# First layer of a two-layer diffusion backbone: values turned by VectorE block transposes and sixteen SBUF transfers a chunk, split on GpSimd

## What is computed

```python
h = x * (1.0 + sc) + sh
hc = ctx * (1.0 + scc) + shc
q, k, v, z = jnp.split(h @ w_in[l], 4, axis=-1)
...
p = jax.nn.softmax(s, axis=-1).astype(v.dtype)
...
return (jnp.einsum('bhwij,bhiwjd->bhwd', p_loc, v_win)
        + jnp.einsum('bhwc,bhcd->bhwd', p[..., n_win:], vc))
...
out = (y * jax.nn.silu(z)) @ w_out[l]
```

## Time and profile before

| what | value |
|---|---|
| median of three runs | 1783.38 us |
| the profiled execution's own time | 1783.56 us |
| its span, first to last instruction | 1781.4 us |
| mean granted TensorE clock | 0.997 of full speed |
| TensorE matmul busy | 1747.2 us, 98% of the span |
| VectorE busy | 1276.3 us, 72% |
| ScalarE busy | 912.5 us, 51% |
| GpSimd busy | 280.0 us, 16% |
| TensorE transposes of values in layer 0 (L687) | 80, 13.5 us busy |

### The profile page before, as it was taken

How to read it: one execution, slowest core, us unless ns; L and a number is a source line. 1 busy time by engine, 2 the same in 40 slices (tenths; PEclk the granted TensorE clock), 3 DMA queues, 4 the chain that set the end, 5 groups by cost and what they waited for, 6 DMA issues and landing times. The chain is left out here.

```text
span 1781.4 us, 30430 instructions
## 1 busy us (share of the span) xinstructions
PE 1747.2 (98%) x10261; PEld 1514.9 (85%) x10261; DVE 1276.3 (72%) x2288; ACT 912.5 (51%) x1638; POOL 280.0 (16%) x245
## 2 busy tenths in 40 slices
PE   7999999999999999999999999999999999999998
PEld 3898989898889898878878889888888888898886
DVE  6677777878787868756878585775848484857658
ACT  4665655555555555640046555564647374654500
POOL 2200000000000000356341010101000010103951
PEclk9999999999999999999999999999999999999999
DMA  9614141414141413316421020202020110102243
GB/s 359 142 37 127 33 120 42 113 47 109 48 109 50 98 52 83 121 57 207 151 83 40 13 62 12 62 0 62 12 62 12 38 36 26 47 12 69 96 155 123
DMA packets 125398, 139.14 MB, mean 78 GB/s; under 512 B 85122, under 2 KB 93474, under 8 KB 125220
## 3 DMA queue, kind: packets, MB, share of 16 engines
q1 hardware_dynamic: 111524, 112.26, 20.7%
q0 software_dynamic: 11088, 16.78, 5.0%
q10 hardware_dynamic: 2736, 9.44, 1.3%
HBM read 107.06 MB, written 17.73 MB: 70 GB/s over the span
## 5 line engine op out<-in xcount | busy, mean ns | idle before, releaser
L676 PE MATMUL acc<-h_hi,w_hi 128*128 128x512 f32 (+1 forms) x1408 | 522.9, 371 | 4.4 <-DVE h_lo L597 3.0
L676 PE MATMUL acc<-h_hi,w_lo 128*128 128x512 f32 (+1 forms) x1408 | 509.1, 362 | 0.0
L676 PE MATMUL acc<-h_lo,w_hi 128*128 128x512 f32 (+1 forms) x1408 | 508.3, 361 | 0.0
L676 PEld LDWEIGHTS acc<-h_hi,w_hi 128*128 128x128 f32 x1408 | 266.2, 189 | 43.4 <-DVE h_lo L597 5.0
L676 PEld LDWEIGHTS acc<-h_hi,w_lo 128*128 128x128 f32 x1408 | 265.7, 189 | 41.9
L676 PEld LDWEIGHTS acc<-h_lo,w_hi 128*128 128x128 f32 x1408 | 266.7, 189 | 34.6
L1841 DVE TENSOR_REDUCE stats<-acc 128x1 f32<-128x1280 f32 x128 | 189.6, 1487 | 38.8 <-PE acc L1948 37.3
L1757 ACT ACTIVATE far_pt<-acc 128x512 f32<-128x512 f32 (+1 forms) x192 | 101.3, 528 | 162.2 <-PE acc L1957 158.8
L1750 ACT ACTIVATE far_prob<-acc,stats 128x1280 f32<-128x1280 f32 x128 | 170.3, 1330 | 24.3 <-DVE stats L1841 22.6
L1948 PE MATMUL acc<-k_dup,q_stack 128*128 128x512 f32 (+1 forms) x768 | 176.7, 367 | 1.8 <-ACT far_prob L1750 0.6
L1447 DVE TENSOR_TENSOR near_pt_lo<-acc,near_pt_hi 128x384 fp32r<-128x384 f32 (+1 forms) x208 | 126.3, 607 | 67.7 <-ACT near_pt_hi L1349 66.8
(11 more groups left out here) (223 smaller groups left out, 2897.5 us busy)
## 6 DMA issues: line engine op xcount, KB each, us to landing
w_raw<-in_w_in SPq DMA_DIRECT2D x64, 512.0 KB, 3.5
near_late_slots<-in_w_mod SPq DMA_DIRECT2D x64, 256.0 KB, 2.8
w_raw<-in_w_out SPq DMA_DIRECT2D x16, 512.0 KB, 3.3
w_raw<-y_t POOLq DMA_DIRECT2D x14, 448.0 KB, 5.1
near_values<-near_values POOLq DMA_DIRECT2D x16, 384.0 KB, 5.7
token_cols<-in_x_cols SPq DMA_DIRECT2D x8, 640.0 KB, 8.9
far_v<-far_v_blocks SPq DMA_DIRECT2D x128, 40.0 KB, 2.0
y_t<-y SPq DMA_DIRECT2D x7, 640.0 KB, 3.0
```

What stands on the lines that cost most here:

```text
L676: mm = nc.tensor.matmul(m.bank(self.bank_of(j, c), w), wt[:, b % 2, k, :], ht[:, k, t0:t0 + w], start=(k == 0 and i == 0), stop=(k == KT - ...
```

## The change

The ten TensorE transposes of a chunk, the six ScalarE copies and the six VectorE subtractions from PSUM go. In their place, as in layer 1: VectorE does three block transposes of `k_raw` at the very start of `dve_part`; SyncE issues sixteen transfers of 32 partitions x 10 x 32 elements, eight ahead of `late.load(2)` and eight behind it; GpSimd then writes the high words (two copies of 128 x 10 x 64) and the low words (two subtractions), ahead of its four transfers. The factor 0.5 moves into the copy out of PSUM. The blocks lie in the memory of the probabilities, so ScalarE waits for GpSimd's split (`p.v_ready`) ahead of a chunk's first exponential.

```diff
         self.prob = sb("prob", [P, 4, LOCAL + CTX])
+        halves = self.prob[:, :, :].rearrange("p b n -> p (b n)")
+        self.v_blocks, self.v_rows = halves[:, 0:TOK], halves[:, TOK:2 * TOK].rearrange("p (t n) -> p t n", n=P)
...
+    def turn_v_blocks(self, v, c):
+
+        for g, (t0, w) in enumerate(GROUPS):
+            v.wait_ge(self.evac, CREDIT + c * self.evacs + (g + 1))
+            self.nc.vector.transpose(self.near.v_blocks[:, t0:t0 + w], self.m.k_raw[:, t0:t0 + w]).then_inc(self.v_turned, 1)
+
+    def spread_v_blocks(self, sp, c, quads):
+
+        sp.wait_ge(self.v_turned, CREDIT + c * self.NV + self.NV)
+        blocks = self.near.v_blocks.rearrange("p (t r n) -> p r t n", r=QUADS, n=BLOCK)
+        for q in quads:
+            for r in range(QUADS):
+                sp.dma_start(self.near.v_rows[r * BLOCK:(r + 1) * BLOCK, :, q * BLOCK:(q + 1) * BLOCK],
+                             blocks[q * BLOCK:(q + 1) * BLOCK, r]).then_inc(self.v_spread, 16)
...
+    def split_values(self, pool, c):
+        pool.wait_ge(self.v_spread, CREDIT + (c + 1) * 16 * QUADS * QUADS)
         for h in range(2):
...
+            src, hi, lo = self.value_parts(h)
+            self.nc.gpsimd.tensor_copy(hi, src).then_inc(self.v_hi, 1)
         for h in range(2):
...
+            src, hi, lo = self.value_parts(h)
+            pool.wait_ge(self.v_hi, CREDIT + c * 2 + h + 1)
+            self.nc.gpsimd.tensor_tensor(lo, src, f(hi), ALU.subtract).then_inc(self.v_ready, 1)
...
     def pe_part(self, pe, c, ring_free, gate_bank_free, late, first):
 
-        ring_free(pe, 0)
-        self.turn_v(pe, c, 0)
-        ring_free(pe, 1)
-        self.turn_v(pe, c, 1)
         if first:
...
         late.reduce(pe, c, 7)
-        self.turn_v(pe, c, 2)
+        ring_free(pe, 0)
+        ring_free(pe, 1)
...
     def dve_part(self, v, c, last, late):
+        self.turn_v_blocks(v, c)
         self.split_lo_part(v, self.nc.vector, c, 2)
-        self.values_lo(v, c, 0)
-        self.values_lo(v, c, 1)
...
                     if not last:
                         p.load_next(sp, c, (4,))
+                    p.spread_v_blocks(sp, c, (0, 1))
                     late.load(sp, c, 2)
+                    p.spread_v_blocks(sp, c, (2, 3))
                     late.store_row(sp, c)
...
                 for c in range(NCH):
+                    p.split_values(pool, c)
                     for shift in range(len(SHIFTS)):
...
                     p.act_part(act, c, lambda e: e.wait_ge(y_ready, CREDIT + c * COLS), last, late)
+                    act.wait_ge(p.v_ready, CREDIT + c * 2 + 2)
```

More of the change, by code:

```diff
@@ L619, in __init__ @@
         lat_only = l == DEPTH - 1
+        self.v_scale = 1.0 if lat_only else 0.5
         self.q_groups = 2 if lat_only else 3
@@ L679, in product_part @@
             mm.then_inc(self.proj, 1)
[L681 to L689, removed]
     def evacuate(self, act, c, j):
@@ L699, in evacuate @@
         self.nc.scalar.activation(dst[:, t0:t0 + w], self.m.bank(self.bank_of(j, c), w), ACT.Copy,
-                                  scale=SCALE if b == 2 else 1.0).then_inc(self.evac, 1)
+                                  scale=(self.v_scale, 1.0, SCALE)[b]).then_inc(self.evac, 1)
     def duplicate_k(self, act, c, h):
@@ L734, in __init__ @@
         self.v_moved = [stack.enter_context(nc.semaphore(f"p0_v_moved{shift}")) for shift in range(len(SHIFTS))]
-        self.v_turns = [(g, range(t0, t0 + w, P)) for g, (t0, w) in enumerate(GROUPS)]
-        self.NV = len(self.v_turns)
-        self.evacs, self.v_parts = 3, 2
+        self.NV = len(GROUPS)
+        self.evacs = 3
+        self.v_spread = self.sem("v_spread")
         self.splits = 2 * (self.cum[2] - 3)
@@ new lines, in spread_v_blocks, with value_parts @@
+    def spread_v_blocks(self, sp, c, quads):
[5 more added lines that the diff above has]
+                             blocks[q * BLOCK:(q + 1) * BLOCK, r]).then_inc(self.v_spread, 16)
+    def value_parts(self, h):
+        parts = self.near.values[:, 0:TOK_TILES, h, :]
+        return self.near.v_rows[:, :, h * HD:(h + 1) * HD], parts[:, :, h * HD:(h + 1) * HD], parts[:, :, (1 - h) * HD:(2 - h) * HD]
@@ L778, in move_values @@
     def move_values(self, pool, c, shift):
-        pool.wait_ge(self.v_ready, CREDIT + c * 2 * self.NV + 4)
+        pool.wait_ge(self.v_ready, CREDIT + c * 2 + 2)
         tiles = self.near.values[:, 0:LAT_TILES, :, :].rearrange("p (b t) h n -> p t b (h n)", t=2)
@@ L859, in act_part @@
         late.take_row(act, c, 7)
-        self.values_hi(act, c, 2)
         self.split_hi_part(act, c, 3)
@@ L879, in dve_part @@
         self.split_x_lo(v, c, 5)
-        self.values_lo(v, c, 2)
         self.split_lo_part(v, self.nc.vector, c, 3)
@@ L1556, in values @@
                             pe.wait_ge(p.gate_done, CREDIT + c * p.q_groups + 1)
-                            pe.wait_ge(p.v_ready, CREDIT + c * 2 * p.NV + 2 * p.NV)
+                            pe.wait_ge(p.v_ready, CREDIT + c * 2 + 2)
                         if u.local and u.shift is not None and j == 0 and u.head == 0:
```

8 lines of the change are left out of this document (removed).

## The result

The changed kernel takes **1789.64 us** (median of 6 runs, 1788.62 to 1793.06) against 1782.78 us (1782.35 to 1783.54) of the kernel before beside it: ratio 1.0041, 95% interval 1.0028 to 1.0054. It is slower by 6.9 us; the forecast was 1789.3 us. Its profiled execution took 1788.99 us with a span of 1787.2 us, 5.8 us longer than the span of before.

A forecast was written before the change was run, and what follows sets the result against it. TensorE, busy 98% of the span, was taken to set the pace. Chunks 1 to 6 at +4.8, chunk 0 at +1.45 and chunk 7 at -0.3 gave +5.95 us: 1789.3 us median, range 1781.0 to 1797.0.

The forecast's parts named there:

- TensorE gives up 1.44 us a chunk: At each chunk's start TensorE loses ten transposes and their wait: 1.44 us a chunk, 11.5 us in eight.
- The transposes make the weight split late; 0.30 remain: VectorE's three block transposes delay the weight split by 1.55 us; product 6 waits 1.14 us, leaving 0.30 us a chunk.
- SP makes piece 3 late, and the query split stands behind its sum: Sixteen transfers on SP delay late piece 3 some 6 us; VectorE's sum and query split follow, putting scores at 173.7 to 174.5.
- 6 x 0.8 for chunks 1 to 6: GpSimd's second subtraction holds VectorE's sum of piece 3, so first scores come 0.8 us later a chunk: 4.8 us.
- Chunk 0, +1.45; chunk 7, -0.3: Chunk 0's first scores come at 83.0 against 81.55; chunk 7, with a shorter SP list, keeps its gain of 0.3 us.
- What costs nothing: First exponential (4 us of cover), GpSimd's shifted transfers, TensorE's ring waits and a second wait behind late scores cost nothing.
- Signs: Expected: product 6 waiting 1.1 us, scores about 1 us; VectorE idle before piece 3's sum; SP issues of 10.5 us a chunk.
- The bounds 1786 to 1795: The forecast's own range in us around 1789.3, the outcome given chance 0.61.
- its own late landing: Upper bound at the first scores: if piece 3's landing takes twice 3.8 us, they start at 178.3, 4.2 us late.
- the sum of 5.95: Whole run: 4.8 us for chunks 1 to 6, +1.45 for chunk 0 and -0.3 for chunk 7, together +5.95 us.
- The third rival: The whole 1.44 us a chunk is kept, needing a weight split that is not late: 1771.9 us, chance 0.05.

The follow-up runs named there:

- the kernel with three edits: Changed kernel with weight split ahead of block transposes, late piece 3 loaded ahead of the last four transfers, output-tile load ahead of the last value split: 1773.69 us.
- the kernel with late subtractions: Changed kernel with GpSimd's two value subtractions waiting, in all chunks but the last, until VectorE has finished the last query split: 1810.98 us.

## Why the prediction was right, and where it was not

**The time and the sign** came out: 1789.3 forecast, 1789.64 measured, slower by over 0.2%. But terms were wrong in opposite directions and cancelled. And the kernel before, beside it, was 0.6 us faster than the 1783.38 that the forecast started from: the change cost 6.9 us, where 5.95 was forecast.

- *TensorE gives up 1.44 us a chunk.* Right: 1.42 us, seen where no new wait stands against it.
- *The transposes make the weight split late; 0.30 remain.* Right. The split ended 154.85 + 1.18 - 147.61 = 8.42 us behind the spread, forecast 154.24 - 145.77 = 8.47; the wait is 0.93 us in chunks 1 to 6 and product 6 comes 0.43 us sooner behind the spread. In chunk 0 it costs 0.25 us, forecast nothing.
- *SP makes piece 3 late, and the query split stands behind its sum.* Right in mechanism: moving either one took the wait away. Issue: 22.7 us behind the spread in chunk 1 and 21.7 in chunk 3, forecast 21.6 to 22.4.
- *6 x 0.8 for chunks 1 to 6.* This is the term that was mis-sized. Chunk 1 paid 1.13, since its second eight transfers took 6.16 us; chunks 2 to 6 paid 0.88 together, 0.18 each, instead of 0.8 each. In chunk 3 the scores came 28.28 us behind the spread, forecast 174.8 - 145.77 = 29.03. The sum was held there, but by 0.37 us (1.78 for 1.41): GpSimd was done at 359.21 - 333.19 = 26.0 us behind the spread, not 26.5, piece 3 landed at the early end of its range, and the held sum ended 1.22 us behind the subtraction (360.43 against 359.21), where the forecast gave it its whole 1.44.
- *Chunk 0, +1.45; chunk 7, -0.3.* +1.72 and -0.14.
- *What costs nothing.* The first exponential did not wait for the values, so that cover held. But the step failed in the last chunk: behind GpSimd's moves I named only the readers of the moved values, and not GpSimd's own next work, the output tiles and weights. It cost 2.1 us of waiting there (3.28 against 1.15, undone by moving one load).

- *Signs.* The waits on the weight split and on the query split, VectorE's idle time that ends with piece 3 and SP's long issue are all there; only the scores' wait in chunks 2 to 6 was 0.3 us and not about 1. The bounds 1786 to 1795 stand in the forecast without a sum: its own late landing, 4.2 us in each of chunks 1 to 6, would have gone beyond them.

So the sum of 5.95 holds 3.1 us too much in chunks 2 to 6, and 3.0 too little elsewhere: 0.27 in chunk 0, 0.33 in chunk 1, 0.16 in chunk 7 and 2.2 behind it. The agreement to 0.3 us is partly luck. The mechanisms and the sign are not: with the last chunk's loss undone the kernel was still slower, 1787.76 us and 1.0027 of before. The third rival, all of 1.44 us kept, is what the kernel with three edits reaches but for chunk 0: 1773.7 us, forecast for it 1771.9.

**Open.** In chunks 2 to 6 the changed kernel's pitch of 92.33 us is 0.36 above 90.74 plus the two waits of 0.93 and 0.30 us. The kernels between tell where: the wait for the weight split alone costs 91.75 - 90.74 = 1.01 us (piece 3 early), 0.08 more than its 0.93, and the scores' wait costs 92.33 - 91.75 = 0.58, 0.28 more than its 0.30. Of this 0.10 is seen in the scores themselves, where the first two take 0.61 us behind a wait and 0.51 without one. The rest fits the overlap of matmuls: without a wait the first scores start 0.16 us ahead of the end of the matmul before them (264.72 against 264.49 + 0.39), and idle time is counted only from that end. What sets the landing of piece 3 in chunk 0 was not tried.

## What to carry to other kernels

When work leaves the engine that sets the pace, list what its new engines and queues do next in every stage, the last one too: here the gain of 11.4 us was there from the start, and three neighbours ate it. Moving a few lines (a weight split ahead of the transposes, a load ahead of the last transfers, a tile load ahead of a value split) brought 9.3 us of it back; the rest is mainly chunk 0. Issue the transfer that someone waits for ahead of a burst of small ones in the same queue. And count GpSimd's subtractions as VectorE's time wherever an operation of VectorE on two SBUF tensors stands beside them.

## What the runs showed of the hardware

- **GpSimd holds VectorE, and order decides what is held.** A subtraction of 128x640, some 1.6 us, held a VectorE operation on two SBUF tensors by up to 1.4 us: pairs of operations of 1.41 us took 2.73, 2.74 and 3.81 us, a weight split of 1.22 us took 2.58. A gating product of 0.41 us took 2.54 beside out-weight subtractions of 2.4 us. The query split, which reads one of its two tensors from PSUM, was not held: with both of VectorE's orders changed its operations ran inside GpSimd's subtractions in chunks 1 to 7 and took their 0.42 to 0.43 us. The Trainium skill (SBUF — State Buffer, section "SBUF: two separate sides") says that whoever of the two starts first has the shared pair of ports for the whole instruction; these rows agree. GpSimd was stretched in turn, 4.11 us for a pair that took 3.09.
- **A wait of TensorE of 2 us can cost nearly twice.** Behind waits of 2.16, 2.49 and 2.56 us the granted clock was 0.57 to 0.63 in the 4 us from about their end on, a mix of the two levels 1.2 and 2.4 GHz; behind 1.38, 1.50 and two of 2.14 us it stayed at 1.00. The fall cost 1.5 and 1.7 us in the two places where it could be told. The length of one wait does not decide it: the clock fell behind 2.03 us in chunk 6 of the kernel with late subtractions, and in the last chunk of the kernel before it was 0.57 from 756 to 760 us behind waits of 1.38 and 1.15 us, while in the kernel of 1773.69 us it stayed at 1.00 there behind 1.38 and 1.16 us.
- **SP's issue of eight transfers of 40 KB takes 5.2 us**, but 5.97 and 6.16 us for one eight each in chunks 0 and 1 of the changed kernel, where a single issue took 1.25 and 1.55 us instead of some 0.62. Why was not tried.
